# Strassen's block products in the feed-forwards' upward product, with weight sums on GpSimd

## The chip, the cores and the metric

The kernel runs on one core of a Trainium2 chip. The metric is the device time of one launch in microseconds (us); smaller is better. TensorE (PE) does matrix products into PSUM, VectorE (DVE) and ScalarE (ACT) do elementwise work and can read PSUM, GpSimd (POOL) does elementwise work in SBUF, and SyncE (SP) issues the weight loads here.

## What is computed

528 tokens (16 meta tokens and 512 of the input) of width 1024 pass through two layers (a gated DeltaNet, then an mLSTM), each followed by a feed-forward, and then through a second block. The change touches the two feed-forwards alone:

```python
def squared_relu_mlp(h, w_up, w_down):      # w_up 1024 x 4096, w_down 4096 x 1024
    a = jax.nn.relu(h @ w_up)
    return (a * a) @ w_down

h = h + squared_relu_mlp(rms_norm(h, ffn_norm[layer]), ff_up[layer], ff_down[layer])
```

All is float32. A product of that precision is made of three passes: each operand is split into a rounded part "hi" and a rest "lo", and hi\*hi, hi\*lo and lo\*hi are added up in PSUM.

## The kernel before

`up_down` (lines 276 to 454) runs a feed-forward in n = 8 groups of 512 hidden features. Activations lie transposed: features on the 128 partitions, tokens in the free dimension. A group has two upward units and two downward units of weights, each 128 x 2048 floats (1 MB), loaded by SP into a ring of four slots (`load_unit`, line 131). A slot is loaded again when `lo_done` tells that the unit in it four units ago has been split. Each unit is split as a whole: ACT makes `whi` (`split_hi`, line 158), DVE subtracts it from the raw unit to make `wlo` (`split_lo`, line 165), in two split slots.

An upward unit gives two output tiles of 128 features x all tokens, eight k-tiles deep; a downward unit four tiles, four k-tiles deep. `product` (line 196) makes the three passes. In the first feed-forward the 528 tokens are two halves of 264 columns, in two PSUM banks, and each half is a matmul with a weight load of its own. In the second the first 16 tokens are no longer needed, and the 512 others are one matmul of 512 columns. So a group's upward part is 4 tiles x 8 k-tiles x 3 passes = 96 products of all tokens (192 or 96 matmuls), and its downward part 8 x 4 x 3 = 96 as well.

The engines run programs of their own, tied by semaphores. `steps` (line 256) lays them out: `first`, `step(0)`, a loop of three rounds of two steps, `last`. In `step(g)` PE does the upward tiles of group g+1, then the downward tiles of group g. Meanwhile ACT takes an upward tile out of PSUM with a relu (line 463), DVE scales it by the norm's inverse root (`rinv`, line 473), ACT squares it (466) and rounds it to `ahi` (331), and DVE makes `alo` (373). The finished downward tiles are added to `h` by DVE (383). GpSimd does nothing in a feed-forward.

A feed-forward begins with the norm's gain: ACT makes `xhi` of each of eight feature tiles (685), DVE `xlo` (701), then DVE adds the last rows of squares (709). The root itself is put off: it multiplies the activations behind the product. PE starts on group 0's upward tiles as the `xlo` tiles come.

Of the kernel before, what the change touches and what calls it, by code (L numbers as in the profile page):

```python
# [23 lines left out]
P = 128  # L24
# [231 lines left out]
def steps(eng, n, step, first, last):  # L256


    first()
    step(0, 0)  # L260
    loops = (n - 2) // 2 if n > 4 else 0
    if loops:
        with eng.Fori(0, loops) as i:
            step(i * 2 + 1, 1)
            step(i * 2 + 2, 0)
    for g in range(1 + 2 * loops, n - 1):
        step(g, g % 2)
    last()
# [6 lines left out]

def up_down(k, name, n, up_cols, w_down, activate, acc, norm, then, last_norm):
# [4 lines left out]
    u0, t0, loaded, split = k.unit, k.tile, k.loaded, k.split  # L281
    with ExitStack() as ctx:
        sb = lambda nm, shape, dt=F32: ctx.enter_context(nc.sbuf_tensor(f"{name}_{nm}", shape, dt))
        ahi, alo = sb("ahi", [P, 2, 4, T], F32R), sb("alo", [P, 2, 4, T], F32R)
        rows = lambda i, n: k.wide[:, i * T:(i + n) * T].rearrange("p (a t) -> p a t", t=T)
        k.a, k.b = rows(0, 2), rows(2, 2)
        s = Named(
            up_free=k.sem(f"{name}_up_free"), normed=k.sem(f"{name}_normed"), a_ready=k.sem(f"{name}_a_ready"),
            hi=k.sem(f"{name}_hi"), lo=k.sem(f"{name}_lo"), down_free=k.sem(f"{name}_down_free"))
        step_unit = lambda g: u0 + 2 + 4 * g  # L290
        step_tile = lambda g: t0 + 4 + 12 * g
        slot = lambda j: (u0 + 2 + j) % RAW_SLOTS
        up_tile = lambda g: t0 if isinstance(g, int) and g == 0 else step_tile(g - 1)
        def down_tile(g):
            return t0 + 12 * g + (4 if isinstance(g, int) and g == n - 1 else 8)
        norm.open(k, ctx, rows(4, 4))
# [7 lines left out]
        def _(sp):  # L304
# [6 lines left out]
            def step(g, par):  # L311
                for j in range(2):
                    if not (isinstance(g, int) and g == 0 and 2 + j < loaded):
# [8 lines left out]

        @block.scalar
        def _(act):
            def hi_tile(g, m, par):

                act.wait_ge(s.a_ready, 4 * g + m + 1)
                if not (isinstance(g, int) and g < 2):
                    if m == 0:
                        act.wait_ge(k.tile_full, down_tile_end(g - 2))  # L330
                nc.scalar.copy(ahi[:, par, m, k.now], k.a[:, m % 2, k.now]).then_inc(s.hi, 1)
            def down_tile_end(g):
                return t0 + 12 * g + 16
            def ups(g, par, tiles):
                for m in tiles:
                    if not (isinstance(g, int) and g == 0 and m < 2):
                        act.wait_ge(s.lo, 4 * g + m - 1)
                    act.wait_ge(k.tile_full, up_tile(g) + m + 1)
                    activate.act(k, act, s, g, m, k.ps[m])
                    hi_tile(g, m, par)  # L340
            def first():
# [7 lines left out]
                split_hi(k, act, u0 + 2, (u0 + 2) % RAW_SLOTS, t0 + 2)  # L349
                ups(0, 0, (0, 1))  # L350
                split_hi(k, act, u0 + 3, (u0 + 3) % RAW_SLOTS, t0 + 4)
                ups(0, 0, (2, 3))
            def step(g, par):

                split_hi(k, act, step_unit(g) + 2, slot(2), step_tile(g) + 2)
                ups(g + 1, 1 - par, (0, 1))
                split_hi(k, act, step_unit(g) + 3, slot(3), step_tile(g) + 4)
                ups(g + 1, 1 - par, (2, 3))
                split_hi(k, act, step_unit(g) + 4, slot(0), step_tile(g) + 8)
                split_hi(k, act, step_unit(g) + 5, slot(1), step_tile(g) + 12)  # L360
            def last():
                split_hi(k, act, u0 + 4 * n, (u0 + 4 * n) % RAW_SLOTS, t0 + 12 * n - 4)
# [7 lines left out]
        def _(dve):  # L370
            def lo_tile(g, m, par):
# [3 lines left out]
            def ups(g, par, tiles):  # L375
                for m in tiles:
                    activate.dve(k, dve, s, g, m, k.ps[m])
                    lo_tile(g, m, par)
            def one_down(g, j):
                dve.wait_ge(k.tile_full, down_tile(g) + j + 1)  # L380
                if not (isinstance(g, int) and g == 0):
# [3 lines left out]
            def downs(g, tiles):  # L385
                for j in tiles:
                    one_down(g, j)
            def first():
# [4 lines left out]
                for j in range(max(split, 1), 3):  # L393
                    split_lo(k, dve, u0 + j, (u0 + j) % RAW_SLOTS)
                ups(0, 0, (0, 1))
                split_lo(k, dve, u0 + 3, (u0 + 3) % RAW_SLOTS)
                ups(0, 0, (2, 3))
            def step(g, par):
                split_lo(k, dve, step_unit(g) + 2, slot(2))
                ups(g + 1, 1 - par, (0, 1))  # L400
                split_lo(k, dve, step_unit(g) + 3, slot(3))
                ups(g + 1, 1 - par, (2, 3))
                downs(g, range(4))
                split_lo(k, dve, step_unit(g) + 4, slot(0))
                downs(g, range(4, 8))
                split_lo(k, dve, step_unit(g) + 5, slot(1))
            def last():
                for j in range(KD):
                    one_down(n - 1, j)
                    if j == 4:  # L410
# [6 lines left out]
        def _(pe):  # L417
            def up(g, ub, us, par, prev):
                for j in range(2):
                    def free(m, j=j):  # L420
                        if prev is not None:
                            prev(2 * j + m)
                        elif m == 1:
                            pe.wait_ge(norm.log, 1)
                    unit_tiles(k, pe, ub + j, us[j], 8, k.xhi, k.xlo, 2 * j, free,
                               norm.x_ready(k, pe) if prev is None and j == 0 else None)
            def down(g, ub, us, par, prev):
                pe.wait_ge(s.lo, 4 * g + 4)
                for j in range(2):
                    def free(m, j=j):  # L430
                        if j == 0:
                            prev(m)
                        else:
                            pe.wait_ge(s.down_free, 8 * g + m + 1)
                    unit_tiles(k, pe, ub + j, us[j], 4, ahi[:, par], alo[:, par], 0, free)
            def first():
                norm.pe(k, pe)
                up(0, u0, [(u0 + j) % RAW_SLOTS for j in range(2)], 0, None)
            def step(g, par):
                if isinstance(g, int) and g == 0:  # L440
                    freed = lambda m: pe.wait_ge(s.up_free, m + 1)
                else:
                    freed = lambda m: pe.wait_ge(s.down_free, 8 * g - 4 + m + 1)
                up(g + 1, step_unit(g), (slot(0), slot(1)), 1 - par, freed)
                down(g, step_unit(g) + 2, (slot(2), slot(3)), par,
# [3962 lines left out]
```

## Time and profile before

| | us |
|---|---|
| median of three runs | 1929.4 |
| the three runs | 1928.72, 1929.40, 1929.87 |
| span of the profiled execution | 1926.8 |
| first feed-forward, first to last of its matmuls | 614 to 993 |
| second feed-forward | 1241 to 1600 |

The profile shows one execution. Its span leaves out 2.6 us of the median, which lie around the first and the last instruction. In the rows below, a group of instructions is named by its line, its engine and "output<-inputs"; a line can be that of a helper, as 196 is for nearly all matmuls. Rows of a timeline give the start and the time taken in us, with "x2" where two like instructions were merged. A matmul's own duration overlaps with the next one's; the pace of PE is the distance between starts.

### The profile page before, as it was taken

What the parts mean: (1) busy time and instruction counts of PE and PEld (TensorE: products, weight loads), DVE (VectorE), ACT (ScalarE), POOL (GpSimd) and SP (SyncE); (2) the same over time, 40 slices, a digit from 0 to 9 for tenths busy, and PEclk for the clock granted to TensorE, in tenths of its full rate; (3) what the DMA queues carried; (4) which work ended last, traced back from release to release, by engine and by line L of the source; (5) the groups of instructions that cost most, each with busy time, mean ns of one, the idle gap of its engine ahead of it and who ended that gap; (6) DMA issues with size and microseconds to landing.
All of it is one profiled execution on the core that took longest, in us unless ns stands there. A gap on an engine that the chain in (4) does not pass through costs nothing. (4 is left out here: it accounts for less than half of the span.)

```text
span 1926.8 us, 31281 instructions
## 1 busy us (share of the span) xinstructions
PE 1864.7 (97%) x12690; PEld 1674.5 (87%) x12690; DVE 1069.8 (56%) x1739; ACT 887.8 (46%) x1459; POOL 106.4 (6%) x142
## 2 busy tenths in 40 slices
PE   8999999999899999999999999999999998999998
PEld 7999999899699999999999977788888885787776
DVE  6666699977744444444455276544444446963444
ACT  6557763677732433333344266353333333424662
POOL 0001140000000000000000020000000002000101
PEclk9999999999999999999999999999999998999999
DMA  8223462255432322222232242232322322321101
GB/s 202 85 76 121 125 193 64 65 158 155 122 89 74 102 88 88 87 87 87 88 88 82 56 98 78 89 107 90 107 87 90 106 87 68 110 66 44 44 23 44
DMA packets 209631, 179.34 MB, mean 93 GB/s; under 512 B 42544, under 2 KB 181808, under 8 KB 209512
## 3 DMA queue, kind: packets, MB, share of 16 engines
q1 hardware_dynamic: 209512, 177.68, 31.1%
q8 instruction: 83, 1.36, 0.3%
q14 instruction: 36, 0.29, 0.0%
HBM read 164.10 MB, written 13.54 MB: 92 GB/s over the span
## 5 line engine op out<-in xcount | busy, mean ns | idle before, releaser
L165 DVE TENSOR_TENSOR main_wlo<-raw,main_whi 128x2048 fp32r<-128x2048 f32 x98 | 225.7, 2303 | 303.9 <-ACT main_whi L158 303.9
L158 ACT CAST main_whi<-raw 128x2048 fp32r<-128x2048 f32 x98 | 186.6, 1904 | 365.8 <-PE ps L196 365.6
L196 PE MATMUL ps<-ffn_xhi,main_whi 128*128 128x264 f32 (+1 forms) x768 | 206.1, 323 | 5.4 <-DVE ffn_xlo L701 5.4
L196 PE MATMUL ps<-ffn_xlo,main_whi 128*128 128x264 f32 (+1 forms) x768 | 206.3, 323 | 0.0
L196 PE MATMUL ps<-ffn_alo,main_whi 128*128 128x264 f32 (+1 forms) x768 | 205.8, 322 | 0.0
L196 PE MATMUL ps<-ffn_xhi,main_wlo 128*128 128x264 f32 (+1 forms) x768 | 205.6, 322 | 0.0
L196 PE MATMUL ps<-ffn_ahi,main_wlo 128*128 128x264 f32 (+1 forms) x768 | 205.1, 321 | 0.0
L196 PE MATMUL ps<-ffn_ahi,main_whi 128*128 128x264 f32 (+1 forms) x768 | 204.6, 320 | 0.0
L196 PE MATMUL ps<-gdn_xhi,gdnf_whi 128*128 128x264 f32 x768 | 160.9, 291 | 4.2 <-DVE gdnf_wlo L1305 4.2
L196 PE MATMUL ps<-gdn_xlo,gdnf_whi 128*128 128x264 f32 x768 | 156.4, 285 | 0.0
L196 PE MATMUL ps<-gdn_xhi,gdnf_wlo 128*128 128x264 f32 x768 | 156.2, 285 | 0.0
L196 PEld LDWEIGHTS ps<-ffn_xhi,main_whi 128*128 128x128 f32 x768 | 128.5, 189 | 17.8 <-issue 6.2
L196 PEld LDWEIGHTS ps<-ffn_xlo,main_whi 128*128 128x128 f32 x768 | 128.2, 189 | 11.4 <-issue 0.2
L196 PEld LDWEIGHTS ps<-ffn_ahi,main_whi 128*128 128x128 f32 x768 | 127.8, 188 | 11.6
L196 PEld LDWEIGHTS ps<-ffn_xhi,main_wlo 128*128 128x128 f32 x768 | 128.0, 189 | 10.9
L196 PEld LDWEIGHTS ps<-ffn_alo,main_whi 128*128 128x128 f32 x768 | 127.5, 188 | 11.2
L196 PEld LDWEIGHTS ps<-ffn_ahi,main_wlo 128*128 128x128 f32 x768 | 127.5, 188 | 10.9
L383 DVE TENSOR_TENSOR h<-h,ps 128x528 f32<-128x528 f32 (+1 forms) x128 | 85.6, 692 | 81.1 <-PE ps L196 81.1
L196 PEld LDWEIGHTS ps<-gdn_xhi,gdnf_whi 128*128 128x128 f32 x768 | 121.1, 190 | 5.5 <-DVE gdn_xlo L1292 4.4
L196 PEld LDWEIGHTS ps<-gdn_xlo,gdnf_whi 128*128 128x128 f32 x768 | 120.0, 190 | 0.0
L196 PEld LDWEIGHTS ps<-gdn_xhi,gdnf_wlo 128*128 128x128 f32 x768 | 119.5, 189 | 0.0
L1194 DVE SCALAR_TENSOR_TENSOR gdn_y<-gdnf_pre,gdnf_convw,gdn_y 128x528 f32<-128x528 f32 x96 | 82.6, 862 | 59.7 <-ACT gdn_y L1167 57.3
(523 smaller groups left out, 3687.5 us busy)
## 6 DMA issues: line engine op xcount, KB each, us to landing
raw<-in_ff_up_dram SPq DMA_DIRECT2D x32, 1024.0 KB, 5.4
raw<-in_ff_down_dram SPq DMA_DIRECT2D x32, 1024.0 KB, 5.0
raw<-in_gdn_in_dram SPq DMA_DIRECT2D x24, 1024.0 KB, 5.8
raw<-in_w_in_dram SPq DMA_DIRECT2D x14, 1024.0 KB, 5.3
raw<-in_mlstm_in_dram SPq DMA_DIRECT2D x12, 1024.0 KB, 5.4
raw<-in_gdn_out_dram SPq DMA_DIRECT2D x8, 1024.0 KB, 6.6
gdn_zr<-gdn_z_spilled SPq DMA_DIRECT2D x26, 264.0 KB, 3.0
gdn_v_spilled<-gdn_o SPq DMA_DIRECT2D x16, 264.0 KB, 2.3
```

What stands on the lines that cost most here:

```text
L158: k.nc.scalar.copy(k.whi[:, slot % SPLIT_SLOTS, :], k.raw[:, slot, :]).then_inc(k.hi_done, 1)
L165: eng.tensor_tensor(k.wlo[:, s, :], k.raw[:, slot, :], k.whi[:, s, :].bitcast(F32), ALU.subtract).then_inc(k.lo_done, 1)
L196: mm = pe.matmul(ps[:, b, 0:k.width], w, x[:, half], start=first and n == 0, stop=last and n == 2)
L383: dve.tensor_tensor(parted(k, acc[:, j, k.now]), parted(k, acc[:, j, k.now]), filled(k, k.ps[j % 4]), ALU.add).then_inc(s.down_free, 1)
L1194: dve.scalar_tensor_tensor(out=self.y[:, b, :], in0=self.pre[:, b, i:i + T], scalar=self.w[:, i, j:j + 1], in1=self.y[:, b, :], op0=ALU.mu ...
```

## The change

The upward product of groups 1 to 7 of each feed-forward is made by Strassen's scheme (in Winograd's form). For one upward unit the weights are taken as 2 x 2 blocks (two feature tiles by two halves of the 1024 input features), the activations as 2 x 2 blocks (input halves by token halves of 264 or 256). Seven block products take the place of eight. Each is a "form": 4 k-tiles x 3 passes = 12 matmuls of half the tokens. A group has 14 forms, 168 matmuls. Group 0 stays as it was, and so do all downward products.

- Four of the seven forms take sums of weight blocks (`mixed`). GpSimd makes them (`sums`, `mix`): four `tensor_tensor` of 128 x 512 per unit, eight per group.
- Four forms take sums of activation blocks. They are made once per feed-forward, on GpSimd too (`first`): eight `tensor_scalar` (gain times `h`, 128 x 528 each), then four `tensor_tensor` of 128 x 1056, each waiting for the one before (`t_made` 1 to 4). ACT rounds each (`t_high`), DVE makes the rest (`t_low`); the last one goes over part of `xhi` and `xlo`.
- Weights are split in quarters (128 x 512), eight rooms in a ring. ACT works six quarters ahead of PE (`AHEAD`), DVE five.
- Some forms are added up in PSUM, the others are put together with what ACT has copied out (`keep`, four copies of half the tokens per unit) by DVE (`join`, four per unit), which then does relu and scaling in one (`joined`).
- One loop round less: two rounds of two steps, and steps 5 and 6 written out.

```diff
+UPS = 14
+STEP = UPS + 8
+AHEAD = 6
...
+            def sums(g, ub):
+                for order in range(1, 5):
+                    mix(g, ub, order)
+            def first():
+                pool.wait_ge(norm.lo, KD)
+                for t in range(KD):
+                    pool.tensor_scalar((y_low if t < 4 else y_high)[:, t % 4, k.now], norm.src[:, t, k.now],
+                                       norm.gain[:, t:t + 1], None, ALU.mult).then_inc(s.y_made, 1)
+                pool.wait_ge(s.y_made, KD)
+                pool.tensor_tensor(y_low[:, :, first_half], y_low[:, :, second_half], y_low[:, :, first_half], ALU.subtract)\
+                    .then_inc(s.t_made, 1)
...
+            def first_sums():
+                pool.wait_ge(norm.lo, KD)
+                sums(0, 0)
+                first()
+                sums(0, 1)
...
+                cast_up(0, 0)
+                cast_up(0, 1)
+                for m in range(2):
+                    open_tile(m)
+                squared(0, 0)
+                hi_tile(0, 0, 0)
+                cast_up(0, 2)
+                cast_up(0, 3)
+                squared(0, 1)
+                hi_tile(0, 1, 0)
+                t_high(2)
+                t_high(3)
+                t_high(4)
+                for m in range(2, 4):
+                    open_tile(m)
+                cast_up(0, 4)
+                t_high(6)
+                cast_up(0, 5)
+                squared(0, 2)
+                hi_tile(0, 2, 0)
...
+                low_up(0, 0)
+                low_up(0, 1)
+                activate.dve(k, dve, s, 0, 0, k.ps[0])
+                activate.dve(k, dve, s, 0, 1, k.ps[1])
+                lo_tile(0, 0, 0)
+                low_up(0, 2)
+                low_up(0, 3)
+                lo_tile(0, 1, 0)
+                t_low(2, 1)
+                t_low(3, 2)
+                t_low(4, 3)
+                low_up(0, 4)
+                t_low(6, 4)
+                activate.dve(k, dve, s, 0, 2, k.ps[2])
+                activate.dve(k, dve, s, 0, 3, k.ps[3])
...
+            def up_form(g, i):
+                ub, f = divmod(i, 7)
+                if f == 6:
+                    pe.wait_ge(k.lo_done, step_unit(g) + ub + 1)
+                else:
+                    pe.wait_ge(s.lo_part, PARTS * g + 6 * ub + f + 1)
+                if zero(g) and ub == 0 and f in t_source:
+                    pe.wait_ge(s.t_lo, {2: 1, 3: 2, 4: 3, 6: 4}[f])
...
+                for kt in range(KD // 2):
+                    for x, (w, y) in enumerate(((whi, xhi), (whi, xlo), (wlo, xhi))):
+                        mm = pe.matmul(bank(ub, f), w[:, i % 8, kt, :], y[:, kt, :], start=f in (0, 1, 2, 4) and kt == 0 and x == 0,
```

## Rows read from the trace of the kernel before

**Rows 1.** The page: the span, then busy time, share of it and instructions.
```profile
span 1926.8 us, 31281 instructions
...
PE 1864.7 (97%) x12690; PEld 1674.5 (87%) x12690; DVE 1069.8 (56%) x1739; ACT 887.8 (46%) x1459; POOL 106.4 (6%) x142
```

**Rows 2.** Busy time per engine in stretches: feed-forwards behind their first group, then the first's start.
```profile
640.60:982.00 341.40, 341.40 (x2793) 341.40 (x2792) 145.26 (x148) 109.67 (x120) 0.00 (x0) 1.00 0.28 90
1264.70:1596.00 331.30, 331.30 (x1432) 268.58 (x1430) 146.84 (x153) 113.27 (x125) 0.00 (x0) 1.00 0.29 92
...
616.00:618.00 2.00, 2.00 (x11) 2.00 (x11) 2.00 (x4) 2.00 (x4) 0.00 (x0) 0.50 0.69 263
```

**Rows 3.** Timeline of PE: 264 columns, first and last of a stretch of pairs.
```profile
780.09 0.41 PE L196 MATMUL ps<-ffn_alo,main_whi 128*128 128x264 f32 x2
...
781.56 0.41 PE L196 MATMUL ps<-ffn_xlo,main_whi 128*128 128x264 f32 x2
```

**Rows 4.** Timeline of PE: 512 columns in the second feed-forward, first and 24th.
```profile
1254.76 0.40 PE L196 MATMUL ps<-ffn_xhi,main_whi 128*128 128x512 f32 x1
...
1260.08 0.40 PE L196 MATMUL ps<-ffn_xhi,main_wlo 128*128 128x512 f32 x1
```

**Rows 5.** Timeline of PE in the second block: 256 columns, first and 22nd.
```profile
1653.49 0.28 PE L4166 MATMUL ps<-main_whi,sec_xhi 128*128 128x256 f32 x1
...
1655.99 0.28 PE L4166 MATMUL ps<-main_whi,sec_xhi 128*128 128x256 f32 x1
```

**Rows 6.** Timeline of ACT and DVE where both feed-forwards start.
```profile
613.48 5.53 DVE L701 SCALAR_TENSOR_TENSOR ffn_xlo<-h,gains,ffn_xhi 128x528 fp32r<-128x528 f32 x8 [1.07 <-ACT ffn_xhi L685]
618.92 2.33 DVE L709 TENSOR_TENSOR wide<-wide 128x528 f32<-128x528 f32 x3
...
640.61 1.91 ACT L158 CAST main_whi<-raw 128x2048 fp32r<-128x2048 f32 x1 [2.84 <-PE ps L196]
...
1240.41 5.39 DVE L701 SCALAR_TENSOR_TENSOR ffn_xlo<-h,gains,ffn_xhi 128x512 fp32r<-128x512 f32 x8 [1.05 <-ACT ffn_xhi L685]
...
1264.74 1.90 ACT L158 CAST main_whi<-raw 128x2048 fp32r<-128x2048 f32 x1 [2.33 <-PE ps L196]
```

**Rows 7.** Instructions by line: durations in ns, least, median and most.
```profile
L331 ACT CAST ffn_ahi<-wide x64: 619/628/637, 634.4 to 1562.0; 128x528 fp32r<-128x528 f32 x32, 128x512 fp32r<-128x512 f32 x32
L1226 POOL TENSOR_TENSOR gdn_an<-wide x16: 1067/1069/1643, 37.1 to 215.3; 128x528 f32<-128x528 f32 x16
L1551 POOL TENSOR_TENSOR gdn_y<-gdn_y,gdn_an x8: 1287/1296/2206, 244.5 to 285.2; 128x512 f32<-128x512 f32 x8
L3672 POOL TENSOR_TENSOR sm_nb<-sm_nb,wide x32: 452/457/729, 1678.4 to 1850.2; 128x128 f32<-128x128 f32 x32
```

**Rows 8.** Groups by line: busy us, then mean ns of one instruction.
```profile
L586 POOL TENSOR_SCALAR_AFFINE_SELECT ident<-ones 128x128 f32<-128x128 f32 x1 | 0.3, 292 | 0.1
L3024 DVE TENSOR_TENSOR ml_w<-ml_w,ps 128x256 f32<-128x256 f32 x16 | 6.7, 421 | 5.0 <-ACT ml_vt L2907 4.7
```

**Rows 9.** Timeline of DVE and POOL where they run at the same time.
```profile
154.52 0.76 DVE L1257 SCALAR_TENSOR_TENSOR wide<-wide,gdnh_gain,gdn_an 128x528 f32<-128x528 f32 x1
...
154.84 1.36 POOL L1226 TENSOR_TENSOR gdn_an<-wide 128x528 f32<-128x528 f32 x1 [5.64 <-PE ps L1236]
...
155.45 1.32 DVE L1194 SCALAR_TENSOR_TENSOR gdn_y<-gdnf_pre,gdnf_convw,gdn_y 128x528 f32<-128x528 f32 x1 [0.17 <-ACT gdn_y L1167]
...
1123.65 2.29 DVE L165 TENSOR_TENSOR main_wlo<-raw,main_whi 128x2048 fp32r<-128x2048 f32 x1 [0.73 <-ACT main_whi L158]
1124.56 1.97 POOL L2852 TENSOR_TENSOR ml_w<-ml_w,ml_below 128x256 f32<-128x256 f32 x1 [3.50 <-DMA ml_kp<-ml_keep_rows]
1125.86 0.68 DVE L2999 TENSOR_TENSOR ml_sc<-ml_var,ml_den 128x2 f32<-128x2 f32 x1
```

**Rows 10.** The page's DMA issues: KB each, median us from issue to landing.
```profile
raw<-in_ff_up_dram SPq DMA_DIRECT2D x32, 1024.0 KB, 5.4
```

More of the change, by code:

```diff
@@ L260, in steps @@
     step(0, 0)
[L261 to L265, printed above, removed]
+    loops = (n - 4) // 2
+    with eng.Fori(0, loops) as i:
+        step(i * 2 + 1, 1)
+        step(i * 2 + 2, 0)
     for g in range(1 + 2 * loops, n - 1):
@@ L294, in down_tile @@
-        def down_tile(g):
-            return t0 + 12 * g + (4 if isinstance(g, int) and g == n - 1 else 8)
-        norm.open(k, ctx, rows(4, 4))
+        up_raw = lambda ub: k.raw[:, slot(ub), :].rearrange("p (k n) -> p k n", k=KD)
+        down_raw = lambda j: k.raw[:, slot(j), :].rearrange("p (k n) -> p k n", k=4)
+        block_of = lambda ub, m, ks: up_raw(ub)[:, ks, P * m:P * (m + 1)]
+        bank = lambda ub, f: k.ps[2 * ub + (0, 0, 1, 0, 1, 1, 0)[f]][:, (0, 1, 0, 0, 1, 0, 0)[f], 0:w2]
@@ new lines, in down_tile @@
+            def down_tile(g, q, par):
+                last = isinstance(g, int) and g == n - 1
+                i, u, j, part = down_place(g, q)
+                if q % 4 == 3:
+                    pe.wait_ge(k.lo_done, u + 1)
+                else:
+                    pe.wait_ge(s.lo_part, part)
+                if q >= 4:
+                    pe.wait_ge(s.down_free, 8 * g + q - 4 + 1)
+                elif last:
+                    pe.wait_ge(s.down_free, 8 * g - 8 + 4 + q + 1)
+                elif q % 2 == 0:
+                    pe.wait_ge(s.joined, 8 * g + 4 * (q // 2) + 4)
+                for kt in range(4):
+                    mm = product(k, pe, k.ps[q % 4], whi[:, i % 8, kt, :], wlo[:, i % 8, kt, :], ahi[:, par, kt, :],
+                                 alo[:, par, kt, :], kt == 0, kt == 3)
+                mm.then_inc(k.tile_full, 1)
@@ L439, in step @@
[L439 to L445, printed above, removed]
-                     lambda m: pe.wait_ge(s.up_free, 4 * g + 4 + m + 1))
+                    unit_tiles(k, pe, u0 + j, (u0 + j) % RAW_SLOTS, 8, k.xhi, k.xlo, 2 * j, free,
+                               norm.x_ready(k, pe) if j == 0 else None)
@@ L447, in last, with step @@
+            def step(g, par):
+                for i in range(UPS):
+                    up_form(g, i)
+                pe.wait_ge(s.lo, 4 * g + 4)
+                for q in range(8):
+                    down_tile(g, q, par)
             def last():
-                down(n - 1, step_unit(n - 1), (slot(0), slot(1)), (n - 1) % 2,
-                     lambda m: pe.wait_ge(s.down_free, 8 * n - 16 + 4 + m + 1))
+                pe.wait_ge(s.lo, 4 * n)
+                for q in range(8):
+                    down_tile(n - 1, q, (n - 1) % 2)
@@ L452, in up_down @@
     k.unit += 4 * n
[L453 removed]
+    k.tile += 4 + STEP * (n - 1) + 8
     k.split = 1
```

312 lines of the change are left out of this document (241 added, 71 removed).

## The prediction

> **What bounds the kernel now.** I read the page's head first: PE is busy 97% of the span, DVE 56%, POOL 6% [rows 1]. Then the stretches: from the end of group 0's upward tiles to near the end of each feed-forward PE is busy without a gap, all at a granted clock of 1.00 (2.4 GHz), while DVE is busy 145.3 of 341.4 us and 146.8 of 331.3 [rows 2]. In these stretches only PE's work sets the time, and whatever other engines do costs nothing until PE waits for it. So two questions decide: how much PE time seven forms save, and where PE has to wait for the sums.
>
> **What PE saves.** The pace comes from distances of starts, not from durations. 264 columns: 12 matmuls from 780.09 to 781.56, 0.1225 us each; the stretch crosses from a downward to an upward tile and shows no gap there [rows 3]. 512 columns: 23 distances in 5.32 us, 0.2313 us [rows 4]. 256 columns, each with a weight load of its own: 21 distances in 2.50 us, 0.1190 us [rows 5].
> First feed-forward: a group goes from 192 matmuls to 168. 24 x 0.1225 = 2.94 us, x 7 groups = 20.6 us.
> Second: 96 x 0.2313 = 22.2 us become 168 x 0.1190 = 20.0 us. 2.2 x 7 = 15.5 us. It is less than the first because two matmuls of 256 cost 0.238 and one of 512 costs 0.231.
> Together 36.1 us, if no form waits.
>
> **The start: a serial chain on POOL.** Forms 2, 3, 4 and 6 of the first unit need the activation sums. POOL starts when the last `xlo` is made: 613.48 + 5.53 = 619.0 [rows 6]. It then has four sums of 128 x 512, eight scalings of 128 x 528 and four sums of 128 x 1056, and ACT has the `t_high` in its queue ahead of the tiles 2 and 3 and of quarters 4 and 5. So the last activation sum, `t_made` 4, sets when form 4 may start, and all behind it.
> How long POOL takes depends on DVE. In the trace the two exclude each other when both read two SBUF operands: a POOL sum that starts at 154.84 while DVE runs until 155.28 ends at 156.20, 0.92 us after DVE and not 1.07; DVE's next, begun at 155.45, ends 0.57 us after POOL, having taken 1.32 instead of some 0.76. At 1124.56 POOL's small sum takes 1.97 us behind a split that ends at 1125.94, and a DVE instruction of two columns waits for it, 0.68 us long [rows 9]. So the two take turns, and the turns add up.
> The Trainium skill says the same (SBUF — State Buffer, Who interferes with whom): a DVE instruction with two SBUF inputs and a GpSimd instruction that reads SBUF block each other for the whole instruction. By that rule, the trace agrees, each sum stays a turn of its own.
> POOL's turns: 528 columns 0.92 [rows 9]; 512 columns between 0.9 and 1.15 (medians of 1.07 and 1.30 alone [rows 7], less the 0.15 that hide in a wait), taken 1.05, in the middle. 1056 columns two of these, 1.84 to 2.3, taken 2.05. The scaling reads one operand and no wide row shows it. A select with one input of 128 columns takes 0.292 [rows 8], a sum of that width 0.457 [rows 7], 0.64 of it: 0.64 x 1.05 = 0.7, bounded by 0.45 (all of it only half a sum) and 1.15 (a whole sum). 4 x 1.05 + 8 x 0.7 + 4 x 2.05 = 18.0 us.
> The Trainium skill (GPSIMD Engine Reference, Engine selection) calls one-input work "roughly line-rate"; at its 1.2 GHz that would be an estimate of 0.45 us for 528 columns, and the chain 2 us shorter than mine. No row here shows it.
> DVE's turns within that time: the rest of three norm sums 1.7 [rows 6], one split 2.1 (2.29 [rows 9], less what hides), eight instructions of one tile (quarters 0 to 3 `low_up`, two scalings, two `alo`) at 0.57 = 4.6, one `t_low` of 1056 columns 1.1. Together 9.5 us. `t_made` 4 falls at 619.0 + 18.0 + 9.5 = 646.5.
> From there DVE is the chain, in turns with POOL's `sums(0, 1)`: `t_low` 3, sum, `t_low` 4, sum, `low_up` 4, sum, `t_low` 6, sum: 3 x 1.1 + 0.55 + 4 x 1.05 = 8.05. Then two scalings and `low_up` 5, 1.85: form 5 starts 9.9 us behind `t_made` 4. Then ACT: square, `ahi`, a kept copy, quarter 6, square, `ahi`, quarter 7, each 0.4 to 0.65 [rows 7], with the subtraction behind: form 7 starts 13.7 us behind it, at 660.2.
> Without waits form 7 would start 7 x 12 x 0.1225 = 10.3 us behind group 0's end at 640.6 [rows 6], at 650.9. The start costs 9.3 us in the first feed-forward.
> In the second the same goes from 1240.41 + 5.39 = 1245.8: + 17.6 + 9.3 = 1272.7, + 13.6 = 1286.3, against 1264.7 + 10.0 = 1274.7. It costs 11.6 us; PE is faster there and POOL isn't.
> Two smaller ones. Quarter 6 frees the slot of the next unit some 11.8 us behind `t_made` 4, it lands 5.4 us later [rows 10], and POOL's next four sums then push DVE's quarters 12 and 13, which have no lead left by then: 1.5 us per feed-forward (0 to 4). And PE, with waits of 2.3 to 3.6 us between forms, may run some of them at half clock, as after the pause before 614 (0.50 from 616 to 618 [rows 2], 1.2 GHz), two microseconds of which cost one: 1.5 us per feed-forward (0 to 3).
> Start in all: 9.3 + 11.6 + 3 + 3 = 26.9 us.
>
> **The steps behind it.** A step of the first feed-forward is 168 + 192 matmuls, 44.1 us. DVE gets 22 quarters, 8 additions to `h`, 4 `alo`, 4 relus, back to back near 0.62 each (618.92 + 2.33 for three [rows 6]), and 8 joins at about 0.42 (one PSUM input [rows 8]): 38 x 0.62 + 3.4 = 27 us, and POOL's eight turns are 8.4 us. 35 of 44. ACT's 22 quarters, 8 copies, 8 others are some 22 us. The tight stretch is the upward one, 20.6 us: DVE needs 14 x 0.62 + 3.4 + 6 x 0.65 = 16, and POOL's first burst there 4.2; the second comes when quarter 13 has been split and the unit has landed, near 20 us into the step, and falls into the downward part, where there is room. DVE may lag by some 4 us at most then, and PE reaches a quarter four forms (5.9 us) after DVE should have started on it. So I cost the steps at nothing. The cover is this lead: if it is gone, each us of lag is a us of PE.
> More waits in PE's queue (one to three per form): nothing, as tile borders with a wait show no gap now [rows 3]. The loads wait for splits a step ahead: nothing. The loop round less: nothing; no wait of PE stands at a loop's end now [rows 2].
>
> **The sum.** 36.1 - 26.9 = 9.2 us gained. Against the profiled span 1926.8 - 9.2 = 1917.6; the median of the runs lies 2.6 us above the span: 1920.2 us.
>
> **The rivals.**
> - The turns cost less than I think, because POOL and DVE overlap. Then `t_made` 4 is at 619.0 + 18.0 = 637, form 7 could start at 647.5, before 650.9, and at 1274 in the second feed-forward, just in time. The whole 36 us are gained: 1893. For it: only few rows show the two at once. Against it: each that does shows full turns [rows 9]. 12%.
> - On the other side: the steps don't hold. If POOL's both bursts fall into the upward part, DVE has 16 + 8.4 = 24.4 us for 20.6, 3.8 too much, and the lead of five quarters doesn't come back because ACT's square waits for DVE's relu and holds ACT's next quarters. This decides as soon as DVE lags by more than 4 forms at any quarter. Priced at 1.5 to 3.8 us in each of 12 steps: 18 to 46 us, 1938 to 1966. For it: DVE goes from 43% busy [rows 2] to 61%, with POOL to 80%. Against it: the loads come a step ahead. 15%.
> - The forms don't run at the pace: 196 forms with a bank change and several waits each, 0.05 to 0.1 us a form: 10 to 20 us less, 1930 to 1940. Against it [rows 3]. 8%.
>
> **How the numbers follow.** My forecast has 65%: 1920, from 1908 (shorter POOL turns, 3 us a feed-forward, no clock loss and no late burst) to 1938 (scalings as long as sums, 5 us a feed-forward, and the smaller terms at their upper ends). A measurement of this kernel tells about 0.2%, 3.9 us, from no change, so faster means under 1925.5, slower over 1933.3. Of the 65%, 47 are faster, 12 same, 6 slower. First rival 12 faster; second 15 slower; third 1 faster, 3 same, 4 slower. Faster 0.60, same 0.15, slower 0.25. The range is from 1900 (part of the first rival out) to 1940 (most of the second out).
>
> **What would show it.** PE: two stretches of waits, near 645 to 660 and 1270 to 1286, ended by DVE (`t_low`, `wlo`), some 9 and 12 us long; no wait after. POOL: `t_made` 4 at about 646, sums of 1.2 to 1.9 us in the timeline with DVE's subtractions 1.3 long beside them. Steps of 44.1 us, then 41.9 us. A wait of PE in the middle of the steps, ended by DVE, would be the second rival; scalings near 0.5 or over 1.1 us would move the start; forms further apart than 1.47 us (264 columns) or 1.43 (256) without a wait would be the third.

## The result, and the profile after

| | before | after |
|---|---|---|
| median of 15 runs each, us | 1929.4 | 1934.2 |
| lowest and highest, us | 1927.9 to 1932.4 | 1930.7 to 1937.2 |
| span of the profiled execution, us | 1926.8 | 1932.1 |
| first feed-forward, first to last matmul, us | 378.2 | 378.0 |
| second feed-forward, us | 356.5 | 363.1 |

The changed kernel is slower by 0.24% (ratio 1.0024, 95% interval 1.0016 to 1.0031), 4.9 us. I had forecast 9.2 us faster. The time lies in the range, but the sign is wrong.

The head of the page after, against [rows 1]: PE is 35 us less busy and the span is longer all the same; DVE and POOL have taken on 189 and 243 us. The clock row (one digit for each of 40 slices, 9 is full speed) has a dent in two slices, one at each start of a feed-forward; the 8 near the end is there before as well.

```profile
span 1932.1 us, 33647 instructions
PE 1829.3 (95%) x13026; PEld 1668.2 (86%) x13026; DVE 1258.7 (65%) x2123; ACT 965.6 (50%) x1787; POOL 349.3 (18%) x278
PEclk9999999999999799999999999979999998999999
```

Where did PE wait? The waits view of PE, first over the first feed-forward (610 to 1000), then over the second (1230 to 1620). Columns: who waited, on whom, us in total, times, longest. The lines of the forms:

```profile
PE ps L670 <- ACT wide L459: 12.7, 1, 12.7
PE ps L670 <- issue: 4.9, 1, 4.9
...
PE ps L670 <- ACT wide L459: 12.3, 1, 12.3
PE ps L670 <- issue: 7.0, 1, 7.0
```

L670 is the matmul of the forms. The forms have two waits at the start of each feed-forward and none behind. The one called "issue" is that of form 2 for `t_low` 1. The other ends with L459, a kept copy on ACT. I had a kept copy in ACT's queue, but no form that waits for it.

The windows view of after gives the same in stretches. Columns: stretch, length, busy time and count of PE, PEld, DVE, ACT, POOL, then the granted clock, DMA share, GB/s.

```profile
641.90:649.70 7.80, 3.03 (x26) 2.82 (x24) 2.47 (x1) 1.07 (x1) 7.56 (x5) 1.00 0.00 0
649.80:652.20 2.40, 2.40 (x12) 2.40 (x12) 0.00 (x0) 0.18 (x1) 2.32 (x2) 0.56 0.00 0
652.40:665.20 12.80, 0.12 (x1) 0.00 (x0) 11.84 (x8) 6.41 (x11) 10.39 (x5) 0.50 0.00 0
665.30:670.60 5.30, 5.30 (x24) 5.30 (x25) 3.73 (x7) 3.72 (x8) 0.00 (x0) 0.50 0.49 136
670.70:700.00 29.30, 29.30 (x242) 29.30 (x241) 23.93 (x34) 14.79 (x28) 12.80 (x8) 1.00 0.37 119
707.20:970.50 263.30, 263.30 (x2162) 263.30 (x2161) 184.53 (x276) 118.66 (x228) 65.25 (x40) 1.00 0.31 97
1330.20:1582.60 252.40, 252.40 (x1585) 227.17 (x1584) 183.25 (x276) 117.69 (x228) 65.11 (x40) 1.00 0.32 101
```

Line by line: forms 0 and 1 at full pace; a wait of 4.9 us; form 2 at a clock of 0.56 (the window holds the starts of its twelve matmuls; it lasts 2.73 us, until 652.52); 12.7 us of waiting, in which DVE is busy 11.84 of 12.80 us; forms 3 and 4 at 0.50 (24 matmuls in 5.4 us, where 2.92 would do); then PE full to the end. The last two rows are six steps of each feed-forward: PE full and the clock 1.00, though DVE is 70% busy and POOL 25%. So the steps hold, and the whole loss lies in some 32 us behind group 0.

What held the forms back is POOL. Its timeline in after, from its first sum on (start, duration):

```profile
620.61 1.69 POOL L377 TENSOR_TENSOR wide<-raw 128x512 f32<-128x512 f32 x1 [278.38 <-DVE ffn_xlo L961]
...
625.81 3.20 POOL L385 TENSOR_TENSOR wide<-raw,wide 128x512 f32<-128x512 f32 x1
628.99 14.56 POOL L393 TENSOR_SCALAR ffn_y<-h,gains 128x528 f32<-128x528 f32 x8
643.64 2.44 POOL L396 TENSOR_TENSOR ffn_y<-ffn_y 128x1056 f32<-128x1056 f32 x1
646.16 2.42 POOL L399 TENSOR_TENSOR ffn_y<-ffn_y 128x1056 f32<-128x1056 f32 x1
648.65 3.33 POOL L402 TENSOR_TENSOR ffn_y<-ffn_y 128x1056 f32<-128x1056 f32 x1
652.06 2.42 POOL L405 TENSOR_TENSOR ffn_y<-ffn_y 128x1056 f32<-128x1056 f32 x1
654.44 2.28 POOL L377 TENSOR_TENSOR wide<-raw 128x512 f32<-128x512 f32 x1
```

The eight scalings (L393) take 14.56 us, where I had 10.2 with DVE's turns among them. `t_made` 4 falls at 654.48, 33.9 us after POOL's start, where I had 27.5. And DVE behind it, with the kept copy that form 3 waits for:

```profile
653.12 4.71 DVE L544 TENSOR_TENSOR ffn_tlo<-ffn_y,ffn_thi 128x1056 fp32r<-128x1056 f32 x2 [3.44 <-ACT ffn_thi L430]
657.76 1.75 DVE L546 TENSOR_TENSOR main_wlo<-raw,main_whi 128x512 fp32r<-128x512 f32 x1
659.43 2.31 DVE L544 TENSOR_TENSOR ffn_xlo<-ffn_y,ffn_xhi 128x1056 fp32r<-128x1056 f32 x1
661.67 2.38 DVE L733 TENSOR_TENSOR wide<-wide,rinv 128x528 f32<-128x528 f32 x2
...
663.52 0.64 ACT L464 ACTIVATE wide<-wide 128x528 f32<-128x528 f32 x1 [4.93 <-DVE wide L733]
...
664.74 0.37 ACT L459 COPY wide<-ps 128x264 f32<-128x264 f32 x1
665.25 0.56 PE L670 MATMUL ps<-ffn_thi,main_whi 128*128 128x264 f32 x1 [12.73 <-ACT wide L459]
```

`t_low` 3, form 3's operand, is there at 655.6. Form 3 starts at 665.25, just behind the kept copy of form 0, which stands in ACT's program behind all of the start: the four `t_high`, the tiles 2 and 3, the quarters 4 and 5, then the square and the rounding of tile 2. ACT stands idle for 4.9 us before that square (L464), until DVE has scaled the tile (L733), and DVE comes to it late because each of its instructions is drawn out beside POOL's second sums. So there are two suspects: the long POOL chain with its turns, and the place of the kept copies.

### The profile page after: what moved, and what is told of

The parts are those of the page before. It is cut to its first block and busy times, and to the rows that moved or that the text cites. A ratio compares the mean times of both kernels' runs of the same rounds, so it can differ in the third digit from the quotient of the medians.

```text
span 1932.1 us, 33647 instructions
## 1 busy us (share of the span) xinstructions
PE 1829.3 (95%) x13026; PEld 1668.2 (86%) x13026; DVE 1258.7 (65%) x2123; ACT 965.6 (50%) x1787; POOL 349.3 (18%) x278
## 5 line engine op out<-in xcount | busy, mean ns | idle before, releaser
L546 DVE TENSOR_TENSOR main_wlo<-raw,main_whi 128x512 fp32r<-128x512 f32 x212 | 164.3, 781 | 15.8 <-ACT main_whi L438 14.0
L377 POOL TENSOR_TENSOR wide<-raw 128x512 f32<-128x512 f32 x28 | 47.1, 1681 | 686.9 <-DVE ffn_xlo L961 354.0
L165 DVE TENSOR_TENSOR main_wlo<-raw,main_whi 128x2048 fp32r<-128x2048 f32 x38 | 90.3, 2377 | 79.0 <-ACT main_whi L158 79.0
L196 PEld LDWEIGHTS ps<-ffn_ahi,main_wlo 128*128 128x128 f32 x768 | 127.5, 188 | 10.9
L670 PE MATMUL ps<-ffn_thi,main_whi 128*128 128x264 f32 (+1 forms) x336 | 98.6, 294 | 36.9 <-ACT wide L459 25.0
L670 PE MATMUL ps<-ffn_xhi,main_wlo 128*128 128x264 f32 (+1 forms) x448 | 126.4, 282 | 0.0
L670 PE MATMUL ps<-ffn_xhi,main_whi 128*128 128x264 f32 (+1 forms) x448 | 126.2, 282 | 0.0
L670 PE MATMUL ps<-ffn_xlo,main_whi 128*128 128x264 f32 (+1 forms) x448 | 126.1, 282 | 0.0
L438 ACT CAST main_whi<-wide 128x512 fp32r<-128x512 f32 x112 | 69.3, 621 | 81.1 <-PE ps L196 81.0
```

The lines of the kernel that those rows point to most:

```text
L165: eng.tensor_tensor(k.wlo[:, s, :], k.raw[:, slot, :], k.whi[:, s, :].bitcast(F32), ALU.subtract).then_inc(k.lo_done, 1)
L196: mm = pe.matmul(ps[:, b, 0:k.width], w, x[:, half], start=first and n == 0, stop=last and n == 2)
L377: mm = pool.tensor_tensor(room(2), block_of(ub, 1, low), block_of(ub, 1, high), ALU.add)
L438: nc.scalar.copy(whi[:, i % 8, :, :], up_weights(ub, f)).then_inc(k.hi_done if f == 6 else s.hi_part, 1)
L546: return dve.tensor_tensor(wlo[:, i % 8, :, :], src, whi[:, i % 8, :, :].bitcast(F32), ALU.subtract)
L670: mm = pe.matmul(bank(ub, f), w[:, i % 8, kt, :], y[:, kt, :], start=f in (0, 1, 2, 4) and kt == 0 and x == 0, stop=kt == KD // 2 - 1 and ...
```

## The experiments

Line numbers in rows of an experiment are those of its own kernel; L669 to L672 are the matmul of the forms in all. "Against after" below is the difference of two ratios to before, each timed against the kernel before in its own series. The feed-forwards' times are first to last matmul in the profiled execution; after has 378.0 and 363.1.

**What the starts hold in all.** The forms read plain `xhi` and `xlo` in place of the activation sums, which are not made:

```diff
-            if f in (2, 3, 4):
-                return thi[:, f - 2, :, 0:w2], tlo[:, f - 2, :, 0:w2]
...
-                first()
...
-                t_high(2)
...
-                t_low(2, 1)
```

> Against the changed kernel: the activation sums are left out (no scalings, no long sums, no t_high and t_low; forms 2, 3, 4 and 6 read the plain xhi and xlo, so the seven products don't give the reference's values). All matmuls, weight sums, quarters, copies and joins stay. It measures what the seven forms save when nothing waits at the start. Theory A (all of the loss is at the two starts, the steps hold): 36 to 38 us less than before, but for a short wait for the kept copies: 1892 to 1895. Rival (part of the loss is in the steps or in forms that don't keep the pace): 1900 or more.

Measured: 1890.7 us, ratio 0.9800 (0.9783 to 0.9818), 38.9 us under the 1929.6 of before; feed-forwards 354.8 and 340.1. The waits view of PE from 608 to 700 keeps one wait, for `xlo` in group 0, 2.7 us as in before and in after, and a stretch of six steps is as full as in after:

```profile
PE ps L196 <- DVE ffn_xlo L948: 2.7, 1, 2.7
```
```profile
684.20:947.00 262.80, 262.80 (x2161) 262.80 (x2161) 184.22 (x276) 118.55 (x228) 66.08 (x40) 1.00 0.30 97
```

I had expected 1892 to 1895. So the forms do give what they should: by their paces the saving is 38.4 us (worked out in the next section). The 43 us by which after lies above this kernel come with the activation sums, and the experiments below divide them.

**Is it the kept copy?** Form 0's copies are put right behind `t_high(2)`:

```diff
+                keep(0, 0, 0, 0, 1, 1)
...
-                    if ub < 2 and f == 0:
+                    if ub < 2 and f == 0 and not (zero(g) and i == 0):
```

> One edit against the changed kernel: in the first step ScalarE copies form 0 out of PSUM (the first kept copy) right behind the first of its four activation-sum casts, not behind all of them and behind the squares of tile 2. Theory A (the start is a serial chain whose last link is an order: form 3 waits at 665.25 for that copy, though its own operand, t_low 3, was there at 655.6): form 3 starts near 655.6, form 4 near 659.5, form 5 with its quarter near 664.7 instead of 670.6, so 5 to 6 us less in each feed-forward, 10 us in all: 1924. Rival B (the chain of GpSimd and VectorE holds form 5 anyhow and the order only hides in it): under 2 us.

Measured: 1932.9 us, ratio 1.0021 (1.0009 to 1.0033), against after 0.03% less, which is nothing, where I had expected 1924; feed-forwards 376.4 and 362.8. The waits of PE from 608 to 700:

```profile
PE ps L671 <- issue: 7.8, 2, 4.9
PE ps L671 <- ACT wide L459: 5.0, 1, 5.0
```

Form 3 now starts 13.9 us behind group 0's end in place of 23.4, and still little is gained: form 5 waits for the next kept copy, until 671.58, and most of the 12.7 us is back in other waits.

Both pairs of copies are therefore moved, form 2's behind `t_high(6)` and `cast_up(0, 5)`:

```diff
+                keep(0, 0, 0, 0, 1, 1)
...
+                keep(0, 0, 2, 1, 2, 3)
```

> Against the changed kernel: both kept copies that forms 3 and 5 of the first step wait for are made early by ScalarE (run e1 moved the first alone and won 1.5 us in the first feed-forward, since form 5 then waited for the second, at 671.6 in that trace). With both, form 5 waits for its quarter alone (668.7 there). Theory A: the order of the two copies is worth 3 to 5 us per feed-forward, 6 to 10 in all: 1926. Rival: VectorE's queue behind t_made 4 sets forms 5 to 7 anyhow: 2 to 3 us in all, 1931.

Measured: 1932.5 us, ratio 1.0013 (1.0002 to 1.0024), against after some 2 us less, which the spread of the two series doesn't tell from nothing; feed-forwards 374.1 and 360.7. No long wait for a kept copy is left from 608 to 700, yet form 7 starts 27.7 us behind group 0's end, against 31.7 in after:

```profile
PE ps L672 <- issue: 7.7, 2, 4.8
PE ps L672 <- DVE main_wlo L548: 3.1, 2, 2.2
PE ps L672 <- ACT wide L459: 0.3, 1, 0.3
```

The kept copy ended the longest wait, but the operands of the forms behind come hardly sooner: form 5 starts 22.9 us behind group 0's end, where its quarter's rest was made 22.8 us behind it in after. And the clock takes back a part. The waits up to form 7 fell from 17.6 to 11.1 us, but four forms in a row (2 to 5) took 2.98 to 3.01 us each, all at a granted clock of 0.50, where after has three slow ones; this costs 6.1 us in place of 3.7. The copies are worth 2 us in time, 6 by the feed-forwards of one execution, out of 43.

**Is it the scaling on POOL?** The eight scalings go to ACT, ahead of its root:

```diff
-                for t in range(KD):
-                    pool.tensor_scalar((y_low if t < 4 else y_high)[:, t % 4, k.now], norm.src[:, t, k.now],
-                                       norm.gain[:, t:t + 1], None, ALU.mult).then_inc(s.y_made, 1)
...
+                for t in range(KD):
+                    nc.scalar.activation((y_low if t < 4 else y_high)[:, t % 4, k.now], norm.src[:, t, k.now], ACT.Copy,
+                                         scale=norm.gain[:, t:t + 1]).then_inc(s.y_made, 1)
```

> One edit against the changed kernel: the eight scalings by the norm's gain are made by ScalarE in its free time in front of the norm's root (8 x 0.65 us, from about 622.2 to 627.4), not by GpSimd, which took 1.60 us for each (14.6 us with VectorE's turns). Theory A: GpSimd's own time for the scalings is what my sum had too small; t_made 4 comes at about 643 instead of 654.5, everything behind it moves by 11.5 us, in both feed-forwards: 23 us less, 1911. Rival B (the turns of VectorE and GpSimd carry the loss, and VectorE's eight subtractions and scalings then hit the four long sums instead): t_made 4 near 648, 6 us per feed-forward, 1922.

Measured: 1915.2 us, ratio 0.9919 (0.9902 to 0.9936), against after some 20 us less; feed-forwards 368.0 and 353.5. `t_made` 4 falls at 640.8, 19.5 us behind POOL's start in place of 33.9: 14.4 us sooner. A feed-forward gains only 10 of them, and the time lies between the two theories: DVE's eight instructions of one tile, which took from 631.0 to 637.4 in after, now lie beside the long sums and take from 631.7 to 648.1. Two waits of the forms remain from 608 to 700:

```profile
PE ps L669 <- issue: 3.9, 1, 3.9
PE ps L669 <- ACT wide L455: 3.5, 1, 3.5
```

Nearly half of what the starts lose comes with the scalings on POOL. What of them is dear? First, the operand that gives one number per partition; a constant 1.5 takes its place (the gain is left out of the activation sums):

```diff
-                                       norm.gain[:, t:t + 1], None, ALU.mult).then_inc(s.y_made, 1)
+                                       1.5, None, ALU.mult).then_inc(s.y_made, 1)
```

> One edit against the changed kernel: the eight scalings on GpSimd multiply by a constant instead of a gain read per partition, so the activation sums are of the plain activations times 1.5 (the gain is left out there). It measures the disputed price. If the per-partition operand is what costs, the instruction falls from 1.60 us to 0.7 to 0.9 us, and the run by 6 us per feed-forward to about 1922. If GpSimd's one-input work is that slow by itself, it stays at 1.60 us and 1934. In both cases Theory A holds that the time follows t_made 4 us for us.

Second, the kind of instruction; `tensor_tensor` with the gain broadcast takes its place:

```diff
-                    pool.tensor_scalar((y_low if t < 4 else y_high)[:, t % 4, k.now], norm.src[:, t, k.now],
-                                       norm.gain[:, t:t + 1], None, ALU.mult).then_inc(s.y_made, 1)
+                    pool.tensor_tensor((y_low if t < 4 else y_high)[:, t % 4, k.now], norm.src[:, t, k.now],
+                                       norm.gain[:, t:t + 1].to_broadcast([P, k.now.stop - k.now.start]), ALU.mult).then_inc(s.y_made, 1)
```

> One edit against the changed kernel: the eight scalings on GpSimd are written as tensor_tensor with the gain broadcast along the tokens, same values. It measures the price again: the scaling with one tensor input took 1.60 us (1.53 with a constant), a sum of two tensors of 528 columns 1.07 in the trace of before. If the two-input instruction is the quicker one whatever it reads, it takes 1.1 to 1.3 us here, 2.5 to 4 us less per feed-forward, about 1927. If a GpSimd pass over 528 columns costs 1.6 in this place, it stays at 1.6 and 1934.

The durations of the scaling's line (least, median, most in ns), in after, with the constant, and as `tensor_tensor`:

```profile
L393 POOL TENSOR_SCALAR ffn_y<-h,gains x16: 1557/1614/2274, 629.0 to 1267.1; 128x528 f32<-128x528 f32 x8, 128x512 f32<-128x512 f32 x8
```
```profile
L393 POOL TENSOR_SCALAR ffn_y<-h x16: 1484/1530/1699, 627.1 to 1260.7; 128x528 f32<-128x528 f32 x8, 128x512 f32<-128x512 f32 x8
```
```profile
L393 POOL TENSOR_TENSOR ffn_y<-h,gains x16: 1034/1488/1531, 633.7 to 1267.8; 128x528 f32<-128x528 f32 x8, 128x512 f32<-128x512 f32 x8
```

Measured: 1931.0 us, ratio 1.0011 (1.0000 to 1.0022), with the constant; 1930.2 us, ratio 1.0001 (0.9989 to 1.0013), as `tensor_tensor`. Some 2.5 and 4.4 us less than after, the first of them hardly more than the noise. At 528 columns an instruction takes 1.60 us in after, 1.53 with the constant and 1.51 as `tensor_tensor`, none near the 0.7 that I took. So the price of the seven is in neither the operand nor the kind. One instruction is cheap, though: as `tensor_tensor`, the first of the eight takes 1.06 us (at 633.75, right behind the sums) and 1.03 in the second feed-forward, and the seven behind it 1.51 to 1.53 and 1.48 to 1.49. So a pass from `h` can cost what POOL's sum of 528 columns took in the kernel before (1.07 [rows 7]). Why the others cost nearly half more stays open.

**Are the turns of DVE and POOL real?** In the critical 20 us DVE makes the operands that PE waits for, while POOL makes sums that are needed only for the second unit. Here POOL waits with them until `t_lo` 4:

```diff
                 first()
+                pool.wait_ge(s.t_lo, 4)
                 sums(0, 1)
```

> One edit against the changed kernel: GpSimd begins the second unit's weight sums of the first step only when VectorE has made the last t_low, so none of the four lies between VectorE's instructions behind t_made 4. Theory of turns (VectorE and GpSimd exclude each other): VectorE's nine instructions there lose four turns of 1.05 us; form 3 starts at about 661 instead of 665.25, 4 us less per feed-forward, 8 in all: 1926. If turns are not what stretches that piece, nothing: 1934.

Measured: 1925.8 us, ratio 0.9983 (0.9970 to 0.9996), some 8 us under after, as expected; feed-forwards 373.6 and 359.5. Not one instruction is removed. DVE's `t_low` of form 4, which took 2.21 us beside POOL's second sums, takes 1.26. The long wait of form 3 falls from 12.7 to 9.0 us:

```profile
PE ps L671 <- ACT wide L460: 9.0, 1, 9.0
PE ps L671 <- issue: 4.9, 1, 4.9
```

**Do the parts add up, and in which order?** Scalings on ACT, tiles 2 and 3 and quarter 4 between the `t_high`, both kept copies early, DVE's scalings between its `t_low`:

```diff
                 t_high(2)
+                open_tile(2)
                 t_high(3)
+                open_tile(3)
+                cast_up(0, 4)
                 t_high(4)
...
+                keep(0, 0, 0, 0, 1, 1)
...
+                keep(0, 0, 2, 1, 2, 3)
...
                 t_low(2, 1)
+                activate.dve(k, dve, s, 0, 2, k.ps[2])
                 t_low(3, 2)
+                low_up(0, 4)
                 t_low(4, 3)
-                low_up(0, 4)
+                activate.dve(k, dve, s, 0, 3, k.ps[3])
```

> Against the kernel with the scalings on ScalarE (1915.2, 0.9919 of the kernel before), the order of the start is changed as well: ScalarE takes tiles 2 and 3 out and makes quarter 4 between the activation-sum casts, and copies form 0 and form 2 out (kept 1 and 2) as soon as they can be there, ahead of the squares; VectorE scales tiles 2 and 3 between its t_low. With the first copy alone moved (run e1) form 5 merely waited for the second one at 671.6. Theory A: with both moved, PE waits for operands only; forms 3 and 4 run while VectorE is still at work, form 7 comes 3 to 5 us earlier in each feed-forward: 1907. Rival: VectorE's instructions, held for 2.8 us each by GpSimd's long sums in e2, are the chain, and the order gives under 1 us: 1914.

Measured: 1908.8 us, ratio 0.9883 (0.9862 to 0.9904); feed-forwards 363.1 and 348.3. With the scalings gone from POOL the order, which is more than the kept copies, is worth another 7 us (with intervals of 3 and 4 us on the two). One wait for `t_low` 1 is left near each start, 5.4 and 4.9 us. To shorten it, POOL starts its first sums without waiting for `xlo`, and its first long sum waits for four scaled tiles only:

```diff
             def first():
-                pool.wait_ge(s.y_made, KD)
+                pool.wait_ge(s.y_made, 4)
...
             def first_sums():
-                pool.wait_ge(norm.lo, KD)
```

> On top of e5: GpSimd doesn't wait for the last xlo before the first unit's weight sums, which need only the landed weights (they then run from about 613.5 to 621, beside VectorE's eight xlo), and its first activation sum waits for the four low scaled tiles only. The long sums then lie between 625 and 637, mostly before VectorE has anything to do (631), so that t_low 2 to 4 are there before PE gets to forms 2 to 4 (from 643.5). Theory A: nearly nothing of the start's 21 and 23 us is left, at most 3 us per feed-forward: 1895 to 1898. Rival (exclusion only moves): VectorE's xlo are held by GpSimd's sums and PE waits in group 0 instead, 4 us or more per feed-forward, 1903 or later.

Measured: 1904.9 us, ratio 0.9862 (0.9839 to 0.9884); feed-forwards 361.7 and 346.5. 4 us of median more, with intervals that overlap, and not the 1895 to 1898 that I expected: the rival was right. The 5.4 us wait is down to 0.2, but PE now waits 1.8 us within group 0 for the split of its unit (L165), which took 4.53 us beside POOL's long sums, for 3.38 in after. Part of the wait was only moved.

**One pair for POOL against DVE.** If each long sum of POOL holds DVE back for nearly its whole time, it is no help that another engine does it. In both kernels the scalings are on ACT, the kept copies early, the first three `t_high` ahead of the first quarter, and POOL's `sums(0, 1)` wait for the `t_low` of form 4. In the first the four long sums are DVE's, right behind the split; in the second the same four are POOL's.

```diff
+            def t_sums():
+                dve.wait_ge(s.y_made, KD)
+                dve.tensor_tensor(y_low[:, :, first_half], y_low[:, :, second_half], y_low[:, :, first_half], ALU.subtract)\
+                    .then_inc(s.t_made, 1)
...
+                t_sums()
+                t_low(2, 1)
+                t_low(3, 2)
+                t_low(4, 3)
```

> Scalings on ScalarE, kept copies early, and now the four long activation sums on VectorE instead of GpSimd, in VectorE's pause from about 628 to 633; their casts follow at once, ahead of quarter 0, and GpSimd makes the second unit's weight sums only behind t_low 4. If VectorE and GpSimd exclude each other, a long sum on GpSimd costs VectorE more (2.8 us per turn, as run e2 showed) than making it itself (1.25 us per instruction of 1056 columns). Expected: forms 2 to 4 find their operands, the start costs under 1.5 us per feed-forward, 1892 to 1895, beside 1890.7 of the run without activation sums. If the two engines only disturb each other a little, it is no better than run e6: 1905.

```diff
-                dve.tensor_tensor(y_low[:, :, first_half], y_low[:, :, second_half], y_low[:, :, first_half], ALU.subtract)\
+                pool.tensor_tensor(y_low[:, :, first_half], y_low[:, :, second_half], y_low[:, :, first_half], ALU.subtract)\
```

> The same kernel as the one with VectorE's long sums, in all orders, but the four long sums stay on GpSimd. The pair differs in the engine of four instructions per feed-forward alone. With exclusion: the long sums take 2.4 to 2.8 us each from about 629 on, last near 640, and VectorE's quarter 0 and all behind it come 7 us later: 4 to 6 us more per feed-forward than its twin, about 1904. Without exclusion the sums lie beside VectorE's work and the pair agrees within 2 us.

Measured: on DVE 1900.3 us (5 above what I expected), ratio 0.9851 (0.9834 to 0.9868), feed-forwards 359.1 and 345.2; on POOL 1913.5 us, 0.9913 (0.9896 to 0.9929), 364.7 and 350.0. The medians are 13.2 us apart, of which the feed-forwards of the two profiled executions show 5.6 + 4.8, within the 4 to 6 each that I expected. In these two the first feed-forward begins 3.3 us apart, ahead of anything in which the kernels differ, so 10 us is the better figure for the change itself. The four sums in the timelines, DVE's and then POOL's:

```profile
626.83 2.32 DVE L532 TENSOR_TENSOR ffn_y<-ffn_y 128x1056 f32<-128x1056 f32 x1
629.19 1.26 DVE L535 TENSOR_TENSOR ffn_y<-ffn_y 128x1056 f32<-128x1056 f32 x1
630.48 1.26 DVE L538 TENSOR_TENSOR ffn_y<-ffn_y 128x1056 f32<-128x1056 f32 x1
631.78 1.26 DVE L541 TENSOR_TENSOR ffn_y<-ffn_y 128x1056 f32<-128x1056 f32 x1
```
```profile
631.34 2.46 POOL L392 TENSOR_TENSOR ffn_y<-ffn_y 128x1056 f32<-128x1056 f32 x1
633.88 2.48 POOL L395 TENSOR_TENSOR ffn_y<-ffn_y 128x1056 f32<-128x1056 f32 x1
636.43 3.36 POOL L398 TENSOR_TENSOR ffn_y<-ffn_y 128x1056 f32<-128x1056 f32 x1
639.87 2.48 POOL L401 TENSOR_TENSOR ffn_y<-ffn_y 128x1056 f32<-128x1056 f32 x1
```

6.1 us on DVE, 10.8 on POOL. So the pair tests more than the turns: undisturbed, such a sum takes 1.26 us on DVE and 2.42 on POOL, and four of them are 4.6 us longer there even without a turn. The rest of the 5.6 us can be turns (two of DVE's `t_low` take 2.52 us beside POOL's sums, in place of 1.25). And the waits of the forms from 608 to 700, in the first kernel and in the second:

```profile
PE ps L672 <- ACT wide L442: 1.1, 2, 0.7
PE ps L672 <- DVE main_wlo L547: 0.7, 1, 0.7
```
```profile
PE ps L672 <- DVE main_wlo L548: 6.6, 2, 4.0
```

The kernel with the sums on DVE beats both kernels: 1.5% under before, 1.7% under after. It is the answer to where the gain went, since it has the same forms and the same weight sums on POOL. 9.6 us above the kernel without activation sums are left.

## Why the prediction was wrong

Of the 14.1 us between forecast and result, the two starts account for +17.8, the forms for -2.3, and what lies outside the feed-forwards for -1.0; 0.4 is rounding and the spread between one execution and the median.

**What PE saves: right.** 12 matmuls of a form take 1.459 us (0.1216 each) and 1.415 us (0.1179), a little less than the 0.1225 and 0.1190 of [rows 3, 5]. The saving is 38.4 us (7 x (192 x 0.1225 - 14 x 1.459) + 7 x (96 x 0.2313 - 14 x 1.415)) for my 36.1, and the kernel without activation sums gains 38.9. The third rival is out.

**The steps hold: right.** They last 43.9 and 42.1 us, for 44.1 and 41.9. The 41.9 was a slip of mine, 42.2 by my own figures. PE is full in the six that the windows show in each feed-forward, and the waits views have no wait of a form behind the starts, so the second rival is out: whatever lag DVE had, it never reached PE.

**The scaling's term: this step failed.** I took 0.7 us, between 0.45 and 1.15, from a select of 128 columns scaled up. It measures 1.60, outside my bounds: eight make 12.8 us for 5.6, 7.2 too few. The error was the upper bound. I had set "a whole sum" as the most that an instruction with one input may cost, and no row showed that. By my own sum, 1.60 in place of 0.7 adds 7.2 us to each start: 1920.2 + 14.4 = 1934.6, close to what was measured, and this term alone turns the sign. That the sum then lands so near is luck: what else I had wrong nearly cancels out. No run shows the chain with scalings of 0.7 us; with none of them on POOL the kernel gained 20 us. The Trainium skill (GPSIMD Engine Reference, Engine selection) calls one-input work "roughly line-rate", by my estimate 0.45 us here; the trace has 1.60 and the measurement decides.

**DVE's turns: the mechanism right, the sizes mixed.** Between its turns POOL's long sums took 2.42 us and not 2.05, so this stretch took 10.9 us for 9.3. Beside the scalings I had charged DVE's work at 4.6 us, and it cost some 1.8: three of the eight scalings took 2.13 to 2.27 us, the others 1.60. The one of 1.60 us at 630.60 lets DVE make a quarter's split (0.82 us, 0.68 undisturbed) in its midst. A long sum doesn't. In the kernel with the scalings on ACT, DVE's instructions of one tile take 2.98 us beside the long sums, where one took 0.70 beside a scaling of 2.27 (L733 of after, at 632.37):

```profile
635.06 2.80 POOL L398 TENSOR_TENSOR ffn_y<-ffn_y 128x1056 f32<-128x1056 f32 x1
635.45 2.98 DVE L732 TENSOR_TENSOR wide<-wide,rinv 128x528 f32<-128x528 f32 x1
...
637.94 2.81 POOL L401 TENSOR_TENSOR ffn_y<-ffn_y 128x1056 f32<-128x1056 f32 x1
638.35 2.98 DVE L732 TENSOR_TENSOR wide<-wide,rinv 128x528 f32<-128x528 f32 x1
```

That agrees with the rule that I had weighed (the Trainium skill, SBUF — State Buffer, Who interferes with whom) for the sums, and not with "for the whole instruction" for the scaling at 630.60. The 8 us of the later sums show that the turns count in time. The first rival had `t_made` 4 at 18 us behind POOL's start and the whole 36 us gained; it is out by far. `t_made` 4 came 33.9 us after POOL's start for 27.5: +7.2 own time of the scalings, -2.8 turns among them, +1.6 long sums, +0.4 the first four: 6.4 us.

**What follows `t_made` 4: this step failed too.** I let form 7 start 13.7 us behind it, and it took 19.1 (13.6 and 18.7 in the second feed-forward). I had followed the operands alone, and put "more waits in PE's queue" at nothing. The change has `if f in (3, 5, 6): pe.wait_ge(s.kept, ...)` in `up_form`, and the copies stand in ACT's program behind all of the start. Both were to be found in the diff. The two runs on the copies show that it is the lesser error by itself: with the copies early form 7 still starts 27.7 us behind group 0's end, and the run with the later sums points to POOL's second burst, which takes turns from DVE's last operands.

**The clock: right, and priced too low.** Forms 3 and 4 take 2.78 and 2.60 us in place of 1.46, at a granted clock of 0.50 (1.2 GHz), and form 2 takes 2.73 at 0.56: 3.7 us in the first feed-forward for 1.5, and 3.9 in the second. With the waits themselves, 17.6 and 19.3 us, that is all that the starts lose. This is what the waits cost on top of themselves.

**The late burst: none.** No wait stands behind form 7 in either feed-forward. 1.5 us each were charged for nothing; the loss of lead that I saw there didn't reach PE.

**The total of the starts.** First: form 7 at 673.55, where without waits it would start at 641.86 + 10.2 = 652.1: 21.4 us. Second: 1298.0 against 1274.7: 23.3 us. 44.7 for 26.9. Against a real saving of 38.4 that is the 6.3 us more which the feed-forwards show. The second pays more, for PE is faster there and the chain isn't.

The chances should have said this too. The gain of 36 us rested on seven groups of known pace, the loss on one chain of sixteen serial POOL instructions with DVE's turns between them, of which most had a price without a row. Against a margin of 9 us, an error of 3 us in each of a few terms decides the sign, and 60% for faster was too much. And the bound that failed stood in my own list: "scalings as long as sums" was to be the worst case.

## What to carry to other kernels

Where a change speeds up a steady stretch and adds a serial chain ahead of it, the chain decides. Write down each instruction of it with the row that prices it, and take the upper bound of a price without a row well above its nearest neighbour, above all where it is counted eight times. Follow every wait of the consumer into the queue of the engine that ends it; and before work is moved to an idle engine, ask how long it takes there and whether the two can run at the same time, since here the same four sums made the kernel 10 to 13 us faster on the busy engine (1.26 us each) than on the idle one (2.42).

## What the runs showed of the hardware that I had not expected

- A `tensor_scalar` on GpSimd of 128 x 528 float32 takes 1.60 us, 1.53 with a constant, 1.51 as `tensor_tensor` with a broadcast gain: more than a sum of two such tiles in the kernel before (1.07 [rows 7]). Only the first `tensor_tensor` of eight took 1.06. The cause is open.
- A long GpSimd sum (2.8 us) stretched a VectorE instruction of one tile to 2.98 us; beside a scaling of 1.60 us one took 0.82, and beside one of 2.27 us 0.70. By these rows the two kinds of instruction don't shut DVE out alike.
- After waits of 4.9 and 12.7 us PE's granted clock was 0.56 and then 0.50, for one form and for two; the ones behind ran at 1.00 again. 36 matmuls cost 3.7 us more than at full clock. Shorter waits didn't avoid it: with both kept copies early, after waits of 4.8, 2.9, 0.9 and 2.2 us, four forms ran at 0.50 one after the other, and 48 matmuls cost 6.1 us more.
